# Evacuating and projecting the first two groups of the first token half ahead of the second half's squares

## The reference

```python
mod = cond @ w_ada[l] + b_ada[l]                 # cond = silu(c)
sh1, sc1, gt1, sh2, sc2, gt2 = [m[:, None, :] for m in jnp.split(mod, N_MOD, axis=-1)]
h = rms_norm(x, g_pre_mix[l]) * (1.0 + sc1) + sh1
zin = h @ w_in[l]                                # 3072 columns: conv value and gate, q, f, i, og
```

## Time and profile before

| | |
|---|---|
| median of 3 runs | 1181.74 us |
| the profiled execution, its own time | 1181.24 us |
| its span, first to last instruction | 1179.5 us |
| PE busy | 1141.0 us, 97% |
| DVE busy | 740.5 us, 63% |
| POOL busy | 661.7 us, 56% |
| ACT busy | 306.1 us, 26% |
| chain that ended last | PE 93%, DVE 3%, ACT 1%, DMA 1% |

### The profile page before, as it was taken

One profiled execution on the slowest core, in us unless ns is written; L12 is line 12 of the kernel. 1 busy time (PEld: TensorE's weight loads), 2 busy tenths in 40 slices (PEclk: granted clock), 3 DMA queues, 4 the chain that ended last, 5 costly groups with the idle time before them and its releaser, 6 DMA issues.

```text
span 1179.5 us, 13775 instructions
## 1 busy us (share of the span) xinstructions
PE 1141.0 (97%) x5528; PEld 952.0 (81%) x5528; DVE 740.5 (63%) x893; ACT 306.1 (26%) x460; POOL 661.7 (56%) x388
## 2 busy tenths in 40 slices
PE   2899999999999999999999999999999999999996
PEld 2788888888888888878888888888888888888885
DVE  5986979979997665658745454544444444444447
ACT  5645253362431624341110101010101010101014
POOL 4155343344342550325495959686868677777755
PEclk9999999999999999999999999999999999999998
DMA  9553323232211161211112121212020202020216
GB/s 329 180 159 121 108 76 104 73 107 81 84 33 37 42 234 82 89 37 54 36 36 72 36 72 36 72 35 73 23 84 19 89 19 90 19 89 18 89 42 262
DMA packets 94097, 98.52 MB, mean 84 GB/s; under 512 B 2925, under 2 KB 80978, under 8 KB 94034
## 3 DMA queue, kind: packets, MB, share of 16 engines
q1 hardware_dynamic: 92576, 93.33, 25.2%
q10 hardware_dynamic: 1458, 4.31, 0.9%
HBM read 89.25 MB, written 8.39 MB: 83 GB/s over the span
## 4 chain that ended last, share of the span: by engine, by line
PE 93%; DVE 3%; ACT 1%; SPq 1%; DMA 1%; issue 1%; ACTq 0%; DVEq 0%
PE pair L1717 31%; PE pair L1638 27%; PE pair L1530 24%; PE pair L1566 4%; PE pair L1695 1%; PE pair L1493 1%; DMA x<-in_x 1%; DVE acc L960 1%; SPq L404 1%; PE pair L1580 1%; PE pair L1561 1%; PE pair L1454 1%; PE pair L1442 1%; PE pair L1582 1%; PE pair L1575 1%
## 5 line engine op out<-in xcount | busy, mean ns | idle before, releaser
L1082 DVE SCALAR_TENSOR_TENSOR pair<-u,conv_w_col,pair 128x512 f32<-128x512 f32 x240 | 162.3, 747 | 1.2
L1394 DVE TENSOR_TENSOR yt<-yt,pair 128x1024 f32<-128x1024 f32 x80 | 97.5, 1219 | 95.2 <-PE pair L1638 95.1
L604 POOL TENSOR_TENSOR w_lo<-raw,w_hi 128x1024 fp32r<-128x1024 f32 x66 | 146.6, 2221 | 5.3
L602 POOL CAST w_hi<-raw 128x1024 fp32r<-128x1024 f32 x66 | 68.4, 1036 | 122.0 <-PE pair L1638 52.5
L525 POOL TENSOR_TENSOR w_lo<-raw,w_hi 128x1024 fp32r<-128x1024 f32 x21 | 52.4, 2499 | 103.4 <-ACT w_hi L690 103.4
L1638 PE MATMUL pair<-w_hi,u_hi 128*128 128x512 f32 x352 | 108.6, 390 | 0.3 <-DVE yt L1392 0.3
L1638 PE MATMUL pair<-w_lo,u_hi 128*128 128x512 f32 x352 | 108.4, 389 | 0.0
L1638 PE MATMUL pair<-w_hi,u_lo 128*128 128x512 f32 x352 | 108.4, 389 | 0.0
L604 POOL TENSOR_TENSOR w_lo<-sraw,w_hi 128x1024 fp32r<-128x1024 f32 x38 | 104.2, 2743 | 3.0
L602 POOL CAST w_hi<-sraw 128x1024 fp32r<-128x1024 f32 x38 | 39.4, 1037 | 117.6 <-PE pair L1638 115.9
L536 POOL TENSOR_TENSOR acc<-acc,ada 128x1024 f32<-128x1024 f32 x28 | 67.3, 2403 | 52.4 <-ACT ada L734 51.1
(11 more groups left out here) (260 smaller groups left out, 2581.3 us busy)
## 6 DMA issues: line engine op xcount, KB each, us to landing
ada<-in_w_ada SPq DMA_DIRECT2D x48, 512.0 KB, 4.1
raw<-in_w_ffn_in SPq DMA_DIRECT2D x44, 512.0 KB, 3.9
raw<-in_w_in SPq DMA_DIRECT2D x24, 512.0 KB, 3.9
raw<-in_w_ffn_out SPq DMA_DIRECT2D x22, 512.0 KB, 3.4
x<-in_x SPq DMA_DIRECT2D x8, 512.0 KB, 8.5
raw<-in_w_out SPq DMA_DIRECT2D x8, 512.0 KB, 3.5
x<-in_x SPq DMA_DIRECT2D x4, 1024.0 KB, 8.2
out<-x ACTq DMA_DIRECT2D x8, 512.0 KB, 2.6
```

The source lines that it names most:

```text
L602: me.done(pool.tensor_copy(w_hi[:, g % WS, cols], src[:, cols]))
L604: pool.tensor_tensor(w_lo[:, g % WS, cols], src[:, cols], w_hi[:, g % WS, cols], ALU.subtract).then_inc(w_split, 1)
L1082: i_ = dve.scalar_tensor_tensor(out=dst, in0=src, scalar=w, in1=dst, op0=ALU.mult, op1=ALU.add)
L1394: dve.tensor_tensor(yt[:, i, :], yt[:, i, :], pair[2 + n % 2][:, :], ALU.add).then_inc(y_added, 1)
```

## The change

Four things, in three engines' lists. The sums of kt 0 and 1 go to banks 0 and 2 (`sums_bank`), and `turn_x` of groups 0 and 1 no longer waits for the scale and shift; ACT's evacuation of these groups waits for them instead. ACT evacuates groups 0 and 1 behind the squares of tiles 0 to 3 and ahead of those of tiles 4 to 7. DVE takes their low parts ahead of tile 4. PE projects groups 0 and 1 for the first chunk ahead of `turn_x(2)`, and for the second chunk between `turn_x(2)` and `turn_x(3)`.

```diff
+        def sums_bank(kt):
+            return bank(2 * kt if kt < 2 else 4 + 2 * (kt % 2))
...
                 kt, half = GROUPS[g]
                 act.wait_ge(turned, g + 1)
+                if g < 2:
+                    act.wait_ge(mod0_ready, kt + 1)
                 if g >= 2:
                     act.wait_ge(h_ready, g - 1)
...
-            squares(range(TT))
-            for g in range(16):
+            squares(range(4))
+            full_and_high(0)
+            full_and_high(1)
+            squares(range(4, TT))
+            for g in range(2, 16):
                 full_and_high(g)
...
             scale_shift(0)
             scale_shift(1)
+            low_half(0)
+            low_half(1)
             normalise_x(4)
             other_vectors()
             for i in range(5, TT):
                 normalise_x(i)
-            low_half(0)
-            low_half(1)
             sum_rows(1, range(2))
...
-                if half == 0:
+                if kt >= 2 and half == 0:
                     pe.wait_ge(mod0_ready, kt + 1)
...
-            def project_group(g):
+            def project_group(g, chunks=(0, 1)):
...
-                for n in range(2):
+                for n in chunks:
...
+            project_group(0, [0])
+            project_group(1, [0])
             turn_x(2)
+            project_group(0, [1])
+            project_group(1, [1])
             pe.wait_ge(vec_ready, 2)
             turn_x(3)
-            for g in range(3):
-                project_group(g)
+            project_group(2)
             mod_sums(2)
             mod_sums(3)
             project_group(3)
```

More of the change, by code:

```diff
@@ L970, in scale_shift @@
                 dve.wait_ge(mod0_summed, kt + 1)
-                sums = bank(4 + 2 * (kt % 2))
+                sums = sums_bank(kt)
                 dve.scalar_tensor_tensor(out=gs[:, 0, kt:kt + 1], in0=sums[:, 1:2], scalar=scale_bias[:, kt:kt + 1],
@@ L1464, in mod_sums @@
                     first = s_ * 2 * P + kt % 2 * P
-                    i_ = pe.matmul(bank(4 + 2 * (kt % 2))[:, s_:s_ + 1], acc0[:, kt // 2 % 2, 0, first:first + P],
+                    i_ = pe.matmul(sums_bank(kt)[:, s_:s_ + 1], acc0[:, kt // 2 % 2, 0, first:first + P],
                                    ones[:, 0:1], start=True, stop=True)
```

## The result

| | before | after |
|---|---|---|
| median | 1181.84 us (6 runs, 1181.68 to 1182.56) | 1186.49 us (6 runs, 1185.93 to 1187.41) |
| profiled execution | 1181.24 us | 1185.93 us |
| its span | 1179.5 us | 1184.2 us |

The ratio after to before is 1.004, with a 95% interval of 1.003 to 1.005: slower by 4.7 us, a small change but clear of the scatter. That lies inside the range, but 1.8 us above the likeliest value (1184.7) and within 0.6 us of the first rival's (1187.0).

A forecast was written before the change was run, and what follows sets the result against it. DVE's block 1 row sums were taken to bound the prologue, PE the rest. Their end shifts by +2.83 or +3.19, taken as +3.0: 1181.24 + 3.0 = 1184.24, plus 0.50 for the median, 1184.7 us; range 1182.9 to 1187.4.

The forecast's parts named there:

- the first rival: PE falls back to the slow rate in its longer pause before T1: +5.3 us in all, 1187.0 us, chance 0.25.
- T1: The end of DVE's row sums of block 1, 36.27 before; forecast 39.10 or 39.46, a shift taken as +3.0 us.
- What bounds it: Prologue: DVE's row sums of block 1, not PE's projections, set T1; PE waits 1.16 us for them.
- ACT: Evacuating groups 0 and 1 early takes 2.75 us, 0.8 usable idle; tile 4 starts at 22.77, last root ends 1.89 later.
- DVE and POOL: Around tile 4, DVE's low parts and POOL's weight split exclude each other; tile 7 ends at 29.57 or 29.93, before 28.10.
- my two orders: At 21.77 DVE goes first (tile 4 ends 26.5, tile 7 29.57) or POOL does (tile 7 29.93).
- PE's six matmuls: Second-chunk projections between `turn_x(2)` and `turn_x(3)`: 2.70 us at the slow pitch, on the chain; group 3's low part ends 35.72.
- Nothing there gives the 3.0 back: Behind T1 the lists and PE's work are unchanged, so the whole 3.0 us shift reaches the total.

The follow-up runs named there:

- one_group_early: The changed kernel with only group 0 taken early, group 1 back in its old places and both second-chunk projections behind `turn_x(3)`: 1181.21 us, ratio to before 0.9996.
- second_chunk_later: The changed kernel with the second-chunk projections of groups 0 and 1 moved behind `turn_x(3)`: 1183.94 us, ratio to before 1.0018.
- short_split: The changed kernel with POOL's second subtract, beside tile 4, cut from 1024 to 32 columns: 1186.25 us, ratio to before 1.0035.
- rows_first_pieces: The kernel before, DVE's parameter subtract behind tile 7, block 1's first row sums before low parts 0 and 1, POOL's second split in four pieces: 1181.9 us.
- keep_busy: The changed kernel with 13 matmuls, their result read by nobody, ahead of `mod_sums(2)` in PE's pause: 1185.74 us, ratio to before 1.0029.
- later_and_busy: second_chunk_later with 10 matmuls, their result read by nobody, ahead of `mod_sums(2)`: 1183.05 us, ratio to before 1.001.

## Why the prediction came out as it did

- **What bounds it.** Right: T1 was set by DVE and decided everything behind. The change relieved PE of twelve matmuls before T1, and PE was not the bound.
- **ACT.** Right to 0.1 us: tile 4 at 22.78 (22.77 was worked out), the last root ends at 27.97 (28.06). one_group_early, against second_chunk_later, shows that it is mostly the second group that doesn't fit.
- **DVE and POOL.** Of my two orders the first came: low 0 and low 1 went ahead of POOL, tile 4 waited for POOL and ended at 26.52 (26.5), tile 7 at 29.60 (29.57). short_split shows the cause. By the rule of the Trainium skill ("SBUF — State Buffer", SBUF: two separate sides) a holder keeps the pair to its end; the trace agrees, tile 4 ending 0.55 us behind POOL's subtract, and rows_first_pieces too, where shorter holders make shorter stalls.
- **PE's six matmuls.** Right: 32.49 - 29.79 = 2.70 us at the slow pitch, DVE idle for 1.25 and 1.40 us, T1 at 39.14 (39.10). second_chunk_later gives 1.5 us back on T1.
- **The step that failed** is the sentence "Nothing there gives the 3.0 back", or rather what stands ahead of it: that behind T1 the same work takes the same time. The sum had nothing for it, and it took 2.55 us longer, since PE came out of its longer pause at 1.2 GHz. This was the first rival, with the right place and mechanism and 2.3 us for 2.55, but only a chance of 0.25. Working PE's end (35.1) and T1 (39.1) out side by side, I had the pause of 4 us and took my own sentence, that no row shows what such a pause does to a fast PE, to mean "probably nothing". The rows did show that PE started slow after every early pause, and the only counter-evidence was a pause three times shorter. The Trainium skill's rule ("TensorE: Matmul & The Clock Gate", Part 1, slow by default and lifted by activity) spoke for the fall, and the trace agrees: granted 0.50 from 39 to 44 us. This rival should have had the larger share.
- **Missed as well:** the 0.7 us that came back at 577 us. "Nothing there gives the 3.0 back" was wrong there too, if by less: the bank part of the change goes with another order of DVE and POOL, which no step of mine looked at. With it, 2.87 + 2.55 - 0.7 = 4.7.
- **The number.** The time lies inside the range because the range was drawn around the first rival as well, and by some luck: without the 0.7 us it would be 1187.2, just below the upper end. It doesn't bear out the likeliest value, which stands for the shift of T1 alone: the kernel before plus 2.87 us.

What stays open is when exactly the clock falls. In the profiled executions it stayed over pauses of 0.18 to 1.16 us ahead of the sums and fell at 1.31, 2.00, 2.15, 2.24, 3.70 and 4.04. But behind 1.38 us at 41.56 it stayed in the kernel before, and behind 1.1 us near 358 us it fell in keep_busy, short_split and later_and_busy and stayed in the other nine. It fell within the pause in two of these (the change and short_split) and 0.45 to 2.2 us after work had come back in the others. The length of the last pause alone doesn't decide it. Open is also why ACT starts later at 544 us in every kernel with the bank part.

## What to carry to other kernels

Before work is moved into an engine's idle stretch, lay its start (which may depend on another engine) and its length against the end of that stretch: here 0.8 of 2.75 us fitted, and the rest was pushed in front of the squares on which the chain ran. Ask of an engine that is relieved whether it was the bound; if it wasn't, the relief turns into a pause, and on PE the pause can cost nearly as much again as the delay that made it, through the clock (2.55 us beside 2.87). A stall between VectorE and POOL was shortened here by cutting the holder into pieces (1.29 us at most), not by moving the instruction that is held, since the next one took its place (2.35 us).

## What the runs showed of the hardware that I had not expected

- A PE pause of 1.31 us was followed by a fall of the granted clock to 0.50, and 1.1 us in one place by a fall in three kernels and none in nine others. Such falls cost 0.6 to 2.5 us each in these profiles and may go with a part of the scatter: of 24 runs of the kernel before on one chip, twelve had a mean granted clock of 0.997 or more, and eleven of them took 1180.8 to 1181.5 us (the twelfth 1182.3); the eleven at 0.996 took 1181.8 to 1183.3 us, and one at 0.967 took 1183.7. On another chip, with 33 runs, the groups overlap (1180.7 to 1182.6 against 1181.3 to 1183.5).
- In the first 32 us the profile of the kernel before grants PE a clock of 1.00 while 512 columns take 0.43 us, the pitch that goes with 0.50 later (39 to 44 us above). That early in a profile the pitch of the matmuls is the better witness.
- Two waits added to ACT's list in the prologue go with 0.28 us more between DVE's end and ACT's start at 544 us, and with 0.7 us less from the loop to the end, in nine kernels against three; no run shows the cause.
